# Expert block rows turned by ScalarE and VectorE instead of TensorE; gated rows' transposes in the middle of the gate/up product

## What is computed

```
def run_block(args):
    toks, e = args
    xb = h_pad[toks]
    return (jax.nn.silu(xb @ w_gate[e]) * (xb @ w_up[e])) @ w_down[e]
```

## Time and profile before

| | |
|---|---|
| median of three runs | 2897.02 us |
| span of the profiled execution (no other time of it is listed) | 2897.5 us |
| phase 2, from the first gather to the end | about 945 us |
| TensorE busy | 2851.8 us, 98% |
| VectorE busy | 1575.9 us, 54% |
| ScalarE busy | 816.7 us, 28% |
| GpSimd busy | 871.3 us, 30% |
| mean DMA rate from 1900 us on | 220 GB/s |

### The profile page before, as it was taken

How to read it: one execution, slowest core, us unless ns; L and a number is a source line. 1 busy time by engine, 2 the same in 40 slices (tenths; PEclk the granted TensorE clock), 3 DMA queues, 4 the chain that set the end, 5 groups by cost and what they waited for, 6 DMA issues and landing times.

```text
span 2897.5 us, 38361 instructions
## 1 busy us (share of the span) xinstructions
PE 2851.8 (98%) x12809; PEld 1883.5 (65%) x12809; DVE 1575.9 (54%) x4155; ACT 816.7 (28%) x1550; POOL 871.3 (30%) x1366
## 2 busy tenths in 40 slices
PE   8999999999999999999999999979999999999997
PEld 6776777777767767776777677744444444444443
DVE  5656565556555565556565656563444444444444
ACT  2223232322332232323232323222222222222222
POOL 1021111112111211121112111114656665665665
PEclk9999999999999999999999999989999999999999
DMA  7312121211122111211121211267675667567653
GB/s 308 141 52 72 60 74 52 73 70 63 52 73 76 56 59 66 81 52 59 66 81 52 73 59 66 75 224 266 235 267 186 227 202 253 200 222 274 237 171 124
DMA packets 109623, 369.01 MB, mean 127 GB/s; under 512 B 39497, under 2 KB 41426, under 8 KB 99442
## 3 DMA queue, kind: packets, MB, share of 16 engines
q1 hardware_dynamic: 48946, 252.91, 23.9%
q0 software_dynamic: 60480, 113.57, 11.9%
HBM read 325.09 MB, written 140.33 MB: 161 GB/s over the span
## 4 chain that ended last, share of the span: by engine, by line
PE 97%; DMA 1%; DVE 0%; issue 0%; ACT 0%; SPq 0%; POOL 0%; POOLq 0%; DVEq 0%; ACTq 0%
PE PB L368 24%; PE PB L1591 19%; PE PB L379 16%; PE PB L463 12%; PE SS L1631 9%; PE YB L463 4%; PE TB L1576 2%; PE YB L417 2%; PE TB L357 1%; DMA arena<-in_w_in 1%; PE SS L426 1%; PE TB L440 1%; PE SS L430 1%; PE TB L404 1%; PE YB L1624 1%; PE MB L408 1%
## 5 line engine op out<-in xcount | busy, mean ns | idle before, releaser
L368 PE MATMUL PB<-arena,hT 128*128 128x512 f32 (+2 forms) x2112 | 726.8, 497 | 1.7 <-DVE arena L1118 0.9
L368 PEld LDWEIGHTS PB<-arena,hT 128*128 128x128 f32 x2112 | 397.9, 191 | 270.5 <-issue 222.7
L1591 PE MATMUL PB<-arena,hT 128*128 x1296 | 569.3, 592 | 0.0
L379 PE MATMUL PB<-hT,arena 128*128 128x128 f32 x4224 | 487.2, 276 | 4.4 <-DVE arena L1106 4.4
L379 PEld LDWEIGHTS PB<-hT,arena 128*128 128x128 f32 x4224 | 481.8, 193 | 8.2 <-issue 4.6
L1591 PEld LDWEIGHTS PB<-arena,hT 128*128 128x128 f32 x1296 | 246.1, 190 | 309.8 <-issue 309.8
L1143 POOL TENSOR_SCALAR rs<-sq 128x2 f32<-128x2 f32 (+1 forms) x66 | 14.2, 215 | 1304.2 <-ACT h L735 958.0
L463 PE MATMUL PB<-arena,tT 128*128 128x274 f32 (+1 forms) x1056 | 357.8, 493 | 0.7 <-ACT tT L639 0.7
L1631 PE MATMUL SS<-arena,xdt 128*128 x640 | 287.9, 592 | 0.0
L463 PEld LDWEIGHTS PB<-arena,tT 128*128 128x128 f32 x1056 | 195.5, 190 | 140.8 <-issue 120.5
L808 DVE SCALAR_TENSOR_TENSOR xc<-xT,cols,xc 128x128 f32<-128x128 f32 x792 | 216.8, 347 | 3.5
(11 more groups left out here) (273 smaller groups left out, 3585.7 us busy)
## 6 DMA issues: line engine op xcount, KB each, us to landing
arena<-in_w_expert SPq DMA_DIRECT2D x32, 2048.0 KB
arena<-in_w_expert SPq DMA_DIRECT2D x32, 1024.0 KB
h_rows<-h SPq DMA_DIRECT2D x34, 512.0 KB, 2.7
x_in<-in_x_rows SPq DMA_DIRECT2D x33, 512.0 KB, 4.6
hT<-in_x_cols SPq DMA_DIRECT2D x33, 512.0 KB, 3.7
x_res<-in_x_rows SPq DMA_DIRECT2D x33, 512.0 KB, 5.1
dec<-running_sums SPq DMA_DIRECT2D x33, 512.0 KB, 3.7
first_rows<-bc SPq DMA_DIRECT2D x33, 512.0 KB, 3.9
```

The source lines that it names most:

```text
L368: mm = nc.tensor.matmul(out, hT[u][:, k, :], w_group(name)[:, k, :], start=k == 0, stop=k == KD - 1)
L379: mm = nc.tensor.matmul(PB[b][:, c * P:(c + 1) * P], w_block(name, c)[:, k, :], hT[u][:, k, :], start=k == 0, stop=k == KD - 1)
L1591: mm = nc.tensor.matmul(PB[u][:, :], hT[u][:, k, :], arena[:, bass.ds(slot + k * 2 * DE, 2 * DE)], start=k == 0, stop=k == KD - 1)
```

## The change

For blocks 2 on, TensorE turns no gathered rows. A 128x1024 block is seen as four groups g of 32 rows, each cut into four column quarters q (the columns c*128 + 32q + i, with c in 0..7 and i in 0..31). ScalarE copies the twelve quarters of the groups 0 to 2 from partitions 32g to partitions 32q (`move`, 32x256 each, into `zz` and `btok`), all twelve in one run between the silu and the weighing. VectorE then turns 32x32 blocks: one instruction for groups 0 and 1 (512 elements a partition), one for group 2 (256), and four of 32x256 for group 3, straight from the gathered rows (`turn_last`). The copies `rows0` and `rows1` remain for blocks 0 and 1 only.

TensorE's order becomes: half of the gate/up product of block b+1, the gated rows' transposes of block b, the other half, the down product. The down product alternates between the banks `SS` and `TB`. ScalarE's order becomes squares, `YB` copy, silu, twelve moves, weighing. VectorE's becomes `add_first`, turns, `norm`, `gate`, weighing, residual add. On GpSimd the store of the weighted rows moves from step b to step b+1, ahead of that step's residual, gather, root, `earlier` and `store`.

```diff
-            def step(b):
-                gather(b + AHEAD)
+            def step(b):
+                if b > 0:
+                    keep(b - 1)
+                residual(b)
+                gather(b + GB)
                 if b > 0:
                     pool.wait_ge(s["fin_sq"], b)
                     root_of(1 - b % 2, b)
-                for k in range(2):
-                    pool.wait_ge(s[f"dn_out{k}"], b + 1)
-                rows_to(first_d[:, :], y_buf[b % GB], first_i, b, first_kept)
-                residual(b + 1)
+                earlier(b)
                 if b > 0:
                     pool.wait_ge(s["fin_out"], b)
                     store(b - 1)
-                earlier(b + 1)
...
             def step(b):
-                u = b % 2
-                pe_gate_up(pe, b + 1)
+                weights = pe_weights(pe, b + 1)
                 slot = entry(pe, TAB_SLOT, b, 0, SLOT_AT[2])
...
-                pe_rows(pe, b + 2)
...
+                pe_gate_up(pe, b + 1, weights, 0, 4)
+                pe_hidden(pe, b)
+                pe_gate_up(pe, b + 1, weights, 4, KD)
+                pe_down(pe, b, slot)
...
+            def move(b, n0, n1):
+
+                if n0 == 0:
+                    act.wait_ge(gathered[b % GB], 16 * (b // GB + 1))
+                    after(act, s["rows_turned"], b - 2)
+                for n in range(n0, n1):
+                    g, q = n // 4, n % 4
+                    ins = nc.scalar.activation(moved[g][32 * q:32 * (q + 1), :], quarter(b, g, q), ACT.Copy)
+                if n1 == 12:
+                    ins.then_inc(s["rows_moved"], 1)
...
+            def step(b):
+                if b > 0:
+                    squares(b - 1, b)
+                hidden(b)
+                silu(b + 1)
+                move(b + 3, 0, 12)
+                weigh(b)
...
+            def turn_last(b):
+
+                dve.wait_ge(gathered[b % GB], 16 * (b // GB + 1))
+                dve.wait_ge(s["gu_full"], b)
+                for q in range(4):
+                    ins = V.transpose(hT[b % 2][32 * q:32 * (q + 1), :, 96:128],
+                                quarter(b, 3, q))
+                ins.then_inc(s["rows_turned"], 1)
+
+            def turn_moved(b):
+
+                dve.wait_ge(s["gu_full"], b)
+                dve.wait_ge(s["rows_moved"], b - 1)
+                V.transpose(hT[b % 2][:, :, 0:64].rearrange("p c (g t) -> p g c t", g=2),
+                            zz[:, :].rearrange("p (g c i) -> p g c i", g=2, i=32))
+                V.transpose(hT[b % 2][:, :, 64:96], btok[:, :].rearrange("p (c i) -> p c i", i=32))
...
+            def step(b):
+                if b > 0:
+                    add_first(1 - b % 2, b, 16 * ((b + 1) // 2))
+                turn_moved(b + 2)
+                turn_last(b + 2)
+                if b > 0:
+                    norm(1 - b % 2, b)
+                gate(b + 1)
+                weigh(b)
+                add_x2(b)
```

More of the change, by code:

```diff
@@ L1354, in build, with quarter @@
         hTb = xdt[:, 0:2 * P].rearrange("p (k t) -> p k t", k=2)
+        moved = [zz[:, 0:DE], zz[:, DE:2 * DE], btok[:, :]]
+        def quarter(b, g, q):
+            return g_buf[b % GB][32 * g:32 * (g + 1), :].rearrange("p (c q i) -> p q c i", q=4, i=32)[:, q, :, :]
+        dn_bank = [[SS[:, n, :] for n in range(2)], [flat(TB[n]) for n in range(2)]]
         silu_g = [ycat[:, 0:DE], ycat[:, DE:2 * DE]]
@@ L1520, in earlier, with keep @@
                 rows_of(first_d[:, :], m_buf[b % 2], last_i, b, first_back[b % 2])
-            def store(b):
-                rows_to(y_out, f_buf[b % 2], last_i, b, y_stored[b % 2])
+            def keep(b):
+                for k in range(2):
+                    pool.wait_ge(s[f"dn_out{k}"], b + 1)
+                rows_to(first_d[:, :], y_buf[b % GB], first_i, b, first_kept)
             def root_of(u, n):
@@ L1570, in pe_rows @@
         def pe_rows(pe, b):
-            pe.wait_ge(gathered[b % GB], 16 * (b // GB + 1))
+            pe.wait_ge(gathered[b], 16)
             for k in range(2):
@@ L1580, in pe_weights, with pe_gate_up, pe_hidden, pe_down @@
             return entry(pe, TAB_SLOT, b, 0, SLOT_AT[2]), entry(pe, TAB_NTH, b, 1, NE) * 32
-        def pe_gate_up(pe, b, weights=None):
+        def pe_gate_up(pe, b, weights, k0, k1):
             u = b % 2
[L1585 to L1590, removed]
+            slot, loads = weights
+            if k0 == 0:
+                pe.wait_ge(w_loaded, loads)
+                if b < 2:
+                    for k in range(2):
+                        pe.wait_ge(s[f"gx_out{k}"], b + 1)
+                after(pe, s["rows_turned"], b - 1)
+                after(pe, s["hb_ready"], b - 1)
+            for k in range(k0, k1):
                 mm = nc.tensor.matmul(PB[u][:, :], hT[u][:, k, :], arena[:, bass.ds(slot + k * 2 * DE, 2 * DE)],
                                       start=k == 0, stop=k == KD - 1)
-            mm.then_inc(s["gu_full"], 1)
+            if k1 == KD:
+                mm.then_inc(s["gu_full"], 1)
+        def pe_hidden(pe, b):
+            pe.wait_ge(s["hb_ready"], b + 1)
+            after(pe, s["hbT_out"], b)
+            for k in range(2):
+                mm = nc.tensor.transpose(YBv[:, k, :], hb2[b % 2][:, k * P:(k + 1) * P], ident)
+            mm.then_inc(s["hbT_full"], 1)
+        def pe_down(pe, b, slot):
+            pe.wait_ge(s["hbT_out"], b + 1)
+            for n in range(2):
+                after(pe, s[f"dn_out{n}"], b - 1)
+                for k in range(2):
+                    mm = nc.tensor.matmul(dn_bank[b % 2][n], hTb[:, k, :],
+                                          arena[:, bass.ds(slot + KD * 2 * DE + k * D + n * 512, 512)], start=k == 0, stop=k == 1)
+            mm.then_inc(s["dn_full"], 1)
         def pe_table_rows(pe):
@@ L1675, in act_phase2 @@
             silu(0)
+            move(2, 0, 12)
             used = over_pairs(act, step)
@@ L1690, in gate, with add_first @@
                 V.tensor_tensor(hb2[u], silu_g[u], PB[u][:, DE:], ALU.mult).then_inc(s["hb_ready"], 1)
-            def add_first(u, back):
-                after(dve, first_back[u], back)
+            def add_first(u, n, back):
+                dve.wait_ge(s["x2_added"], n)
+                dve.wait_ge(first_back[u], back)
                 V.tensor_tensor(f_buf[u], f_buf[u], m_buf[u], ALU.add).then_inc(s["first_added"], 1)
@@ L1730, in dve_phase2 @@
             V.memset(spare[:, 3:4], 0.0)
-            add_first(1, 16 * used)
+            add_first(1, 2 * used, 16 * used)
             norm(1, 2 * used)
```

79 lines of the change are left out of this document (27 added, 52 removed).

## The result

The changed kernel takes 2974.84 us, median of four runs (2958.61 to 2983.92). The kernel before took 2897.69 us in four runs beside it. The ratio is 1.026, with a 95% interval of 1.0229 to 1.0292: slower by 77 us. The forecast was 2865 us with a range of 2824 to 2905, so both the sign and the range were missed.

What follows compares the result with a forecast made beforehand. The prediction took TensorE alone to bound each step. From 2897 us it took 70 for row transposes and 2 for the end, and added 40 for expert loads: 2865 us, range 2824 to 2905.

Steps and rivals of the forecast that it cites:

- row transposes off TensorE, with the end: TensorE's step falls from 11.39 to 10.52 us, 70 us over 80 steps; the run's end takes 2 us more off.
- twelve moves: ScalarE's twelve 32x256 copies a step, 0.31 us from one to the next: 3.7 us, bounds 3.4 and 4.9.
- turns: VectorE's six transposes a step, priced like other one-pass operations: 2.5 us, bounds 2.0 and 4.4.
- loop of moves and turns: ScalarE-VectorE loop of moves, weighing, residual add, add_first and turns: 9.6 us, fitting under TensorE's 10.52 us step.
- expert loads: Late gathers beside loads in the expert loop stall TensorE: 17 x 2.2 + 11 x 0.3, say 40 us, ends 0 and 62.
- end of the run by itself: After the last block's products: norm no longer in between, some 0.6 us wait for unused moves; 2 us off.
- `move` waiting for the turns in each: Sign of rival B: every step longer, with ScalarE's moves waiting for VectorE's turns in each.
- rival B: Loop of moves and turns outlasts TensorE's step, by unoverlapped moves or two-cycle transposes: about 2915 or 3000 us; chance 0.20.
- A load that hits costs 9.8 - 7.6 = 2.2 us: Expert loop: data land 9.8 us behind the product's end, add_first must start by 7.6; TensorE loses 2.2 us a load.
- wrong altogether: Sign against the whole prediction: granted clock below 1.00 in the loop, or TensorE waiting for `rows_turned`.
- Rival A: Expert loads hurt less or not at all: 2825 us, up to 2838 if a few hit; chance 0.22.
- Rival C: Loads cost more than 2.2 us; all 28 at 2.5 give back 70 us, 2890 to 2903 us; chance 0.10.

Runs made afterwards that it cites:

- half_moves_small_loads: Changed kernel with six of the twelve moves left out and the last 28 experts' loads cut to 64 columns each: 2827.44 us, ratio to the kernel before 0.9763.
- small_loads: Changed kernel with the gate/up and down loads of the last 28 experts cut to 64 columns each: 2884.43 us, ratio to the kernel before 0.9961.
- half_moves: Changed kernel with six of the twelve moves left out, expert loads whole: 2960.75 us, ratio to the kernel before 1.023.
- late_turns: Changed kernel reordered: ScalarE YB copy, silu, six moves, squares, six moves, weighing; VectorE add_first, weighing, gate, norm, turns, residual add: 2836.65 us, ratio 0.9782.
- copy_first: Changed kernel with the YB copy put back ahead of the squares on ScalarE: 2938.39 us, ratio to the kernel before 1.0143.
- before_squares_first: Kernel before with only the squares put ahead of the YB copy on ScalarE: 2926.5 us, ratio to the kernel before 1.0094.

## Why the prediction was wrong

Its terms, each against the difference of two spans or a row:

| term | predicted | measured |
|---|---|---|
| row transposes off TensorE, with the end | -72 us | -72: span 2825.6 us, 2825.5 foreseen (half_moves_small_loads) |
| twelve moves | 3.7 us (3.4 to 4.9) | 5.12 us |
| turns | 2.5 us (2.0 to 4.4) | 2.83 us |
| loop of moves and turns | 9.6 us, costs nothing | 11.18 us, costs 2882.1 - 2825.6 = 56 us |
| expert loads | +40 us (0 to 62) | 2969.8 - 2882.1 = 88 us |
| end of the run by itself | -2 us | from last down product to last store 12.8 us, before 11.2: +1.6 (in half_moves_small_loads 10.9) |

That the first line comes out to 0.1 us is partly luck: in half_moves_small_loads the end gives back 0.2 us and not 2.

**Right:** what bounded the kernel; TensorE's term; the price of the turns, taken from other one-pass operations (0.704 us for 512 elements a partition, 0.403 for 256); and the path by which a load reaches TensorE, from the gather over `add_first` and the squares to the copy. The prediction also asked what would show it wrong, and named "`move` waiting for the turns in each". That is what the waits show, in 63 of 80 steps here and in all 80 of small_loads.

**First failed step: the moves' price, "I take 0.31, since the shape is that of the row".** The row is a 128x256 operation, and what I took from it was its overlap with its follower. That follower is an accumulator read of one column, not a second copy, so the row could not tell how soon one copy follows another. The moves are as long as that row, 0.414 us, but they do not overlap: 0.427 us from one to the next. Even my high bound of 0.41 was passed. The same went for the four 32x256 turns, 1.79 us for four, where I had let each overlap by 0.07. Together moves and turns take 5.12 + 2.83 = 7.95 us, and the prediction had written down where that leads: no full gain from 7.1 us, slower from 7.9. It is rival B, at 0.20, by the first of its two mechanisms (each move costs what it costs alone). The loop by itself does not make the kernel slower, since weighing, the two adds and the hand-overs take 11.18 - 7.95 = 3.2 us and not 3.45: a step of 11.18 us against 11.39 would give 17 us in 80 steps, and small_loads gains 13.

**Second failed step: "A load that hits costs 9.8 - 7.6 = 2.2 us", times 17.** Three things were off. How often: the load queue's own waits show that 27 of 28 loads now wait for a product, against 17 before.

```profile
SPq L1235 <- PE PB L1603: 193.7, 27, 23.6
```

I had carried a count over from a kernel whose steps the change alters. How late: where `add_first` waits for its rows behind a load, it starts on average 9.4 us after the load was issued before (24 cases), 10.9 us in the changed kernel (26 cases) and 10.8 us in half_moves (27 cases), so 10.9 and not 9.8. With the 10.52 us step the prediction's own rule then gives 10.8 - 7.6 = 3.2 us a load; half_moves shows 89.8 us of waits in 28 cases, 3.2 us each. (The rule had a flaw of its own: it called 7.7 us the soonest start of `add_first` and 7.6 us the latest allowed, so every step would have been late; half_moves_small_loads shows no such wait.) In the longer step of the changed kernel there is more room, and the loads add 96.1 - (16.8 + 15.9) = 63.4 us of waits. And a cost that was not in the sum: **the clock**. The matmuls of the down product, changed kernel and then small_loads (columns: count | busy us, mean ns | idle before):

```profile
L1622 PE MATMUL TB<-arena,xdt 128*128 x320 | 164.1, 661 | 51.3 <-ACT xdt L1690 51.3
L1622 PE MATMUL SS<-arena,xdt 128*128 x320 | 160.8, 650 | 44.8 <-ACT xdt L1690 44.8
```

```profile
L1622 PE MATMUL TB<-arena,xdt 128*128 x320 | 147.8, 605 | 16.8 <-ACT xdt L1690 16.8
L1622 PE MATMUL SS<-arena,xdt 128*128 x320 | 147.7, 604 | 15.9 <-ACT xdt L1690 15.9
```

The same 640 records take 324.9 us instead of 295.5: 29 us, a third of what the loads cost. 63 + 29 = 92 us agree with the 88 of the spans. The prediction had listed a granted clock below 1.00 as something that would make it "wrong altogether", but gave it no price.

**Rival A** fell with the loads' price. The page that it leaned on (the Trainium skill, "DMA: Bandwidth & Descriptors", section "Queues, rings and completion order") lets each DMA engine take turns between its queues. From that I took that a small gather beside a large load would come through early. The trace shows turns between the queues, but no early arrival. The loads go out on queue q1, the gathers on q0 (columns: packets, MB, share of the 16 DMA engines). First 2196 to 2201 us of the changed kernel, behind its load at 2194.4, then 2201 to 2206 us of half_moves, behind its load at 2199.98 and the gather of earlier rows at 2199.44:

```profile
q1 hardware_dynamic: 103, 1.69, 79.5%
q0 software_dynamic: 108, 0.41, 21.6%
```

```profile
q1 hardware_dynamic: 109, 1.79, 95.6%
q0 software_dynamic: 32, 0.01, 0.7%
```

In the first the two queues move about one packet each, of 16 KB and of 4 KB. In the second nearly all that moves is the load, with a gather outstanding. In neither are the rows of `add_first` there before the load is through. The load's own end can be read from its 128 packets: the last one ends 8.4 us behind the load's issue in the kernel before, 9.3 us in the changed kernel and 10.0 us in half_moves (means over the 24, 26 and 27 cases above), and `add_first` starts 1.0, 1.6 and 0.8 us after that, never ahead of it. In those cases the gather was issued between 0.8 us ahead of the load and 2.5 us behind it. Gathers issued later come later: 4.0 us behind the load, `add_first` starts at 11.1 us (late_turns, 14 cases); 6.7 us behind it, at 12.3 us (copy_first, 23 cases). So rows asked for beside a load come with the load's end. Why they do, and why the load itself ends later in the changed kernel than before, is not shown; the new order on GpSimd was not tried by itself.

**Rival C** was right in kind (all loads, over 2.5 us each) but priced at 70 us on its own. What made the kernel slower is B and C together: 56 of loop and 88 of loads, against 72 gained. I had given them separate chances, as if only one could happen, and no case for both. The two share a part, the place of the turns behind `add_first`: it closes the loop, and it carries a late gather on to TensorE (copy_first). The place of the squares ahead of the copy does harm of its own (before_squares_first).

**The end:** `norm` is gone from between, as foreseen, but the last weighing waits for moves that nobody uses, from the down product's end at 2951.61 to 2954.29. I had put 0.6 us on that; it is 2.7.

## What to carry to other kernels

When work is moved from the bounding engine to others, write down the loop that the moved work closes between them, every operation in it, and price it with no overlap as well as with it; a margin of 0.9 us over twelve operations is 0.075 us each, which no row of another shape can secure. Then look at what stands in that loop, or ahead of a hand-over to the bounding engine, that can be late for reasons of its own (here `add_first`, which waits for a gather beside a 2 MB load) and move it out: the same operations in another order took 2836.65 us instead of 2974.84. Change the order on both engines of such a loop in one experiment, since each half alone was worse than either kernel by over 100 us.

## What the runs showed of the hardware

* Back-to-back 32x256 copies on ScalarE (0.414 us long) start 0.427 us apart, and 32x256 transposes on VectorE (0.438 us) 0.45 us apart, while the 128x256 silu of 0.38 us on ScalarE is followed after 0.27 us (2301.34 to 2301.61, late_turns) and a 128x512 transpose of 0.70 us on VectorE after 0.63 us. A quarter of the partitions saves nothing: 0.414 us for a 32x256 copy against 0.41 us for the 128x256 operation of the earlier trace rows, 0.438 us for a 32x256 transpose against 0.403 us for a 128x256 one.
* After a wait of 6.25 us TensorE's down product ran at the lower of its two levels, 1.2 instead of 2.4 GHz: eight records in 6.44 us instead of 3.44, at 2316.34 us, with a granted clock of 0.51 from 2316 to 2322 us. The granted clock of the stretches fell to 0.93 to 0.99 with such waits, and was 1.00 in every stretch shown without them.
* An indirect DMA's issue on GpSimd took 1.02 us or 2.05 us for the same gather: those of the earlier rows went from 1.01 to 1.7 us on average in the changed kernel, those of `x_rows` from 1.57 to 1.75 down to 1.05 to 1.07. What decides between the two was not tested.
